# Low weight halves moved from VectorE to GpSimd, and high halves one block earlier on ScalarE, around the output projections of a two-block transformer kernel

## The chip, the cores and the metric

One NeuronCore of a Trainium2 chip runs the whole program. The metric is the device time of one execution in microseconds (us). The kernel before took 1125.66 us, the median of three runs (1124.29 to 1127.17).

## What is computed

Two transformer blocks over 512 tokens of width 1024, in float32. What matters here is the end of each sublayer: an output projection, a post-norm added to the residual, a pre-norm, and the next matrix product.

```python
h = h + rmsnorm(mix, norm_mix_post[l])            # boundary 0
z = rmsnorm(h, norm_mlp_pre[l]) @ w_up[l]
ff = jnp.square(jax.nn.relu(z)) @ w_down[l]
h = h + rmsnorm(ff, norm_mlp_post[l])             # boundary 1
...
    h = rms_norm(x, pre_norm[layer])
    y = even_mixer(h, ...)  /  odd_mixer(h, ...)
    x = x + rms_norm(y, post_norm[layer])         # boundaries 2 and 3
```

## The kernel before, in words

Every float32 product is made of three fast ones. A number is kept as a high half (rounded to the reduced format) and a low half (the number less its high half), and `mm3` issues high by high, high by low and low by high (lines 702 to 704). So each 1024 x 512 chunk of weights, loaded by SyncE in two pieces of 1 MB into `wl`, is split twice. ScalarE copies the piece into `wh` (`hi(n, piece)`, line 1362, 128x2048). VectorE subtracts it from `wl` and writes the low half over the raw weights as `wlr` (`lo(n, piece)`, line 1768, 128x2048, both inputs in SBUF). TensorE waits for `wlo_done` to reach the count of the piece (`weights`, from `token_tile` and `channel_tile`). There are two slots; chunk n uses slot n % 2, and its load waits until chunk n - 2 has been used.

Chunks are numbered in order of use: N_O1 (second half of the first output projection), then N_UP; the last down chunk, then N_GA; N_AO1, then N_AB. Each pair meets at a boundary, s = 0, 1 and 2. There TensorE makes the projection for four blocks of 128 tokens (24 matmuls each), and for each block b the others do the norms in token-major layout:

- ScalarE (`boundary_blocks`, line 1408): the sum of squares of the block (`half_square`, L1376), the post scale (L1383, L1385), then, in blocks 1 and 2, `hi` of the following chunk, then `pre_scale` (L1391, L1394, L1396: the sum of squares of the new residual and its root), then the high half of the block before, turned (`hi_turned`, L1403).
- VectorE (`boundary_blocks`, line 1826): at s = 1 the last partial sum (`add_down`, L1825), `half_gained` (L1780, from PSUM; at s = 1 L1778, from SBUF), the new residual `rt` (`new_resid`, L1795, 128x1024), in blocks 2 and 3 `lo` of the following chunk, the low half of the block before (`lo_turned`, L1812, from PSUM), and the normed block `un` (`normed`, L1804, 128x1024). L1795 and L1804 read two tensors of SBUF.
- TensorE turns the normed block into channel-major layout (`turn_block`, L840): blocks 0 and 1 inside the tiles of the projection, blocks 2 and 3 inside the tiles of the next chunk at s = 0 and 1 (N_UP, N_GA: token-major products), and by themselves at s = 2, where every tile of N_AB needs all four blocks.

Each engine works through its list in the order in which it is written, and semaphores order the engines. GpSimd has nothing to do at the three boundaries: its list goes from the first mixer's steps to a memset (L1276) before the second mixer's, and from these to the memsets of `glu` (L1282) and the conv sums. Its one subtraction of a whole weight piece is in the first mixer (`split(1)`, L1231, 128x2048). The counter `wlo_done` is bare: it says how many pieces are done and not which, so its increments must come in the order of the pieces.

Of the kernel before, what the change touches and what calls it, by code (L numbers as in the profile page):

```python
# [5 lines left out]
F32 = mybir.dt.float32  # L6
F32R = mybir.dt.float32r
I32 = mybir.dt.int32
ALU = mybir.AluOpType
# [47 lines left out]
N_O0, N_O1, N_UP, N_GA, N_KV, N_Q, N_U, N_GB = 0, 1, 2, 18, 19, 20, 21, 22  # L57
N_AO0, N_AO1, N_AB, N_G0, N_G1, N_CO0, N_CO1 = 23, 24, 25, 29, 30, 31, 32
# [54 lines left out]
def chunk_width(n):  # L113
    return CW if n == N_KV else 2 * CW


def piece_count(n, piece):

    return 2 - piece if n == N_O0 else 2 * n + piece + 1
# [90 lines left out]
def block_kernel(nc, a, out):  # L210
    ctx = ExitStack()
    with ctx:
# [138 lines left out]
        wl = [at("wl0", [P, KT, 512], raw_off), at("wl1", [P, KT, 512], hi_off)]  # L351
        wlr = [at("wlr0", [P, KT, 512], raw_off, F32R), at("wlr1", [P, KT, 512], hi_off, F32R)]
# [852 lines left out]
        @block.gpsimd  # L1205
        def _(pool):
            chain = Chain(pool, pool_step)
            pool.memset(eps[:, :], EPS).then_inc(eps_set, 1)
            pool.wait_ge(eps_set, 1)
            chain.link(pool.memset(relw[32:33, :], -1e30))  # L1210
            pool.memset(gate_w[:, :, :], 0.0).then_inc(gatew_set, 1)
            pool.wait_ge(gatew_set, 1)

            def sum_squares(n):

                for k in range(KT - 1):
                    pool.wait_ge(sq_done, 8 * n + k + 1)
                    if k == 0:
                        if n >= 1:
                            pool.wait_ge(rsum_done, n)  # L1220
                        pool.tensor_copy(sq_sum[:, :], sq[:, k % 2, :]).then_inc(sqsum_done, 1)
                    else:
                        pool.wait_ge(sqsum_done, 7 * n + k)
                        pool.tensor_tensor(sq_sum[:, :], sq_sum[:, :], sq[:, k % 2, :], ALU.add)\
                            .then_inc(sqsum_done, 1)

            def split(c):

                pool.wait_ge(hi_done, c + 1)
                pool.wait_ge(lo_done, c)  # L1230
                pool.tensor_tensor(w_lo[:, c % 2, :, :], raw[:, c % 2, :, :], w_hi[:, c % 2, :, :].bitcast(F32),  # L1231
                                   ALU.subtract).then_inc(lo_done, 1)

            def mixer_step_pool(layer, step):
                what, i = step[0], step[1]
                k = 16 * layer + i
                if what == "gla_scaled":

                    d, t = i % 2, i // 2
                    pool.wait_ge(evac_done, 10 + t)  # L1240
                    pool.wait_ge(eb_done, i + 1)
                    if d == 0:
                        pool.wait_ge(enb_done, i + 1)
                        pool.tensor_tensor(kint(d, t), ka[:, t, :], gx[:, :], ALU.mult).then_inc(kint_done, 1)
                    pool.wait_ge(ek_done, i + 1)
                    pool.tensor_tensor(bb[:, :], ka[:, t, :], gl[:, :], ALU.mult).then_inc(ks_done, 1)
                    if d == 1:
                        pool.wait_ge(ks_done, i + 1)
                        pool.tensor_tensor(kint(d, t), ka[:, t, :], gx[:, :], ALU.mult).then_inc(kint_done, 1)
                elif what == "gla_dS" and i == 0:  # L1250
                    pool.wait_ge(vtok_done, 1)
                    pool.wait_ge(pv_done, STEPS)
                    pool.memset(Am[:, :, :, :], 0.0).then_inc(Am_set, 1)
                elif what == "pool_window":

                    pool.wait_ge(evD_done, evacs_before(TILE_AT[N_U, i], "D") + 1)
                    if i == 0:
                        pool.wait_ge(upad_set, 1)
                        pool.wait_ge(mix2_in, 16 * MIX2_LOADS)
                    else:  # L1260
                        pool.wait_ge(pooled_done, i)
                    src = uu[:, i, :]
                    for m in range(i + 1):
                        sh, lo = 1 << m, (2 << m) - 1
                        dst = wsum[:, m % 2, :]
                        chain.link(pool.tensor_tensor(dst[:, lo:], src[:, lo:], src[:, lo - sh:UPAD + TOK - sh], ALU.add))
                        src = dst
                    pool.tensor_tensor(src[:, UPAD:UPAD + 16], src[:, UPAD:UPAD + 16], wcnt[:, i, :], ALU.mult)\
                        .then_inc(wsum_done, 1)

            split(1)
            sum_squares(0)
            for step in STEPS_OF[0]:
                mixer_step_pool(0, step)
            pool.wait_ge(wtile_done, CHUNK_END[N_GA - 1])
            pool.memset(uu[:, :, 0:UPAD], 0.0).then_inc(upad_set, 1)  # L1276
            for step in STEPS_OF[1]:
                mixer_step_pool(1, step)
            pool.wait_ge(ob_done, 4)

            for slot in range(4):
                pool.memset(glu[:, slot, 0:CPAD], 0.0).then_inc(pad_set, 1)  # L1282
            for t in range(KT):
                for m in range(1, ACT_TAPS + 1):
                    made = PRODUCTS * t + m + 1
                    pool.wait_ge(prod_done, made)
                    g = made - 1
                    if m == 1:
                        if t >= 2:
                            pool.wait_ge(conv_done, t - 1)  # L1290
                        pool.tensor_tensor(pacc[:, t % 2, :], prod[:, (g - 1) % 4, :], prod[:, g % 4, :], ALU.add)\
                            .then_inc(padd_done, 1)
                    else:
                        pool.wait_ge(padd_done, ACT_TAPS * t + m - 1)
                        pool.tensor_tensor(pacc[:, t % 2, :], pacc[:, t % 2, :], prod[:, g % 4, :], ALU.add)\  # L1295
                            .then_inc(padd_done, 1)
# [3 lines left out]
        def _(act):  # L1300
# [57 lines left out]
            def hi(n, piece):  # L1358

                slot, kk, cols = n % 2, slice(4 * piece, 4 * piece + 4), slice(0, chunk_width(n))  # L1360
                act.wait_ge(wraw[slot][piece], 16 * sum(chunk_dmas(q) for q in range(slot, n + 1, 2)))
                act.activation(wh[slot][:, kk, cols], wl[slot][:, kk, cols], ACT.Copy).then_inc(whi_done, 1)  # L1362
# [43 lines left out]
            def boundary_blocks(s, following):  # L1406

                for b in range(NBLK):
                    half_square(s, 1, b)
                    post_scale(s, b)  # L1410
                    if b in (1, 2):
                        hi(following, b - 1)
                    pre_scale(s, b)
                    if b >= 1:
                        hi_turned(s, b - 1)
                hi_turned(s, NBLK - 1)
# [293 lines left out]
        def _(dve):  # L1710
# [53 lines left out]
            def lo(n, piece):  # L1764

                slot, kk, cols = n % 2, slice(4 * piece, 4 * piece + 4), slice(0, chunk_width(n))
                dve.wait_ge(whi_done, piece_count(n, piece))
                dve.tensor_tensor(wlr[slot][:, kk, cols], wl[slot][:, kk, cols], wh[slot][:, kk, cols].bitcast(F32),  # L1768
                                  ALU.subtract).then_inc(wlo_done, 1)
# [37 lines left out]
            def lo_turned(s, b):  # L1807

                for g in range(2):
                    dve.wait_ge(hiT_done, 2 * (NBLK * s + b) + g + 1)  # L1810
                    cols = slice(b * P, (b + 1) * P)
                    dve.tensor_tensor(act_lo[:, 4 * g:4 * g + 4, cols], psT[:, g, :].rearrange("p (k n) -> p k n", k=4),  # L1812
                                      act_hi[:, 4 * g:4 * g + 4, cols].bitcast(F32), ALU.subtract)\
                       .then_inc(loT_done, 1)
# [12 lines left out]
            def boundary_blocks(s, following):  # L1827

                for b in range(NBLK):
                    if s == 1:  # L1830
                        add_down(3, 1, b)
                    half_gained(s, 1, b)
                    new_resid(s, b)
                    if b >= 2:
                        lo(following, b - 2)
                    if b >= 1:
                        lo_turned(s, b - 1)
                    normed(s, b)
                lo_turned(s, NBLK - 1)

            def mixer_step_dve(layer, step):
                what, i = step[0], step[1]
# [386 lines left out]
```

## Time and profile before

| | |
|---|---|
| median of three runs | 1125.66 us |
| the profiled execution | 1125.93 us |
| its span, first to last instruction | 1124.1 us |
| TensorE busy | 1033.6 us (92%) |
| VectorE busy | 584.4 us (52%) |
| ScalarE busy | 468.5 us (42%) |
| GpSimd busy | 170.0 us (15%) |
| mean granted TensorE clock | 0.960 of full |

TensorE is busy nearly throughout, so time is lost where it stands still or runs at the lower clock. Matmuls overlap: one 128x512 matmul is recorded as 0.39 us, and the next starts 0.23 us after it.

### The profile page before, as it was taken

Reading aid. Unit: us, or ns where it says so; the run is one execution under the profiler, and the core shown is the slowest. Engines: PE = TensorE matmul, PEld = TensorE weight load, DVE = VectorE, ACT = ScalarE, POOL = GpSimd, SP = SyncE. Lnnn points to the kernel's source line nnn. Section 1 sums busy time; section 2 is a strip of 40 time slices with the busy share of each in tenths; the row PEclk is TensorE's granted clock in tenths of the full one; section 3 lists DMA queues with packets and bytes.
Section 4 is the critical chain, followed back from the end, with each engine's and each line's share of the span. In section 5 each row is a group of like instructions: output and inputs, shape, how many; then the busy total and the mean of one; then the engine's idle time right before and its main releaser. Section 6 shows DMA issues by size and latency. Waiting matters only on the chain.

```text
span 1124.1 us, 12285 instructions
## 1 busy us (share of the span) xinstructions
PE 1033.6 (92%) x4847; PEld 824.7 (73%) x4847; DVE 584.4 (52%) x768; ACT 468.5 (42%) x765; POOL 170.0 (15%) x131
## 2 busy tenths in 40 slices
PE   3899999997999999999999979989898899979897
PEld 2677677886788888888888868767677667657676
DVE  5436665235744234333344463366556397777853
ACT  3325562135533334134123354234355557556541
POOL 2200101000000000000000000022000189886300
PEclk8999999998999999999999999989999799999989
DMA  6532102034221252233224214302033222210301
GB/s 213 73 122 76 38 1 76 1 113 150 76 76 75 75 187 75 75 109 116 76 75 149 76 38 132 141 1 75 2 136 120 68 76 76 75 54 27 145 1 75
DMA packets 55823, 93.91 MB, mean 84 GB/s; under 512 B 2581, under 2 KB 23958, under 8 KB 55638
## 3 DMA queue, kind: packets, MB, share of 16 engines
q1 hardware_dynamic: 53648, 90.61, 23.3%
q10 hardware_dynamic: 2118, 2.52, 1.6%
q8 instruction: 39, 0.64, 0.2%
q14 instruction: 18, 0.15, 0.0%
HBM read 90.76 MB, written 2.36 MB: 83 GB/s over the span
## 4 chain that ended last, share of the span: by engine, by line
PE 55%; DVE 8%; ACT 4%; issue 3%; POOL 1%; DMA 1%; SPq 0%; DVEq 0%; POOLq 0%; ACTq 0%
PE acc L702 17%; PE acc L703 17%; PE acc L704 16%; DVE wlr L1768 2%; ACT wh L1362 2%; DVE psT L2113 1%; POOL pacc L1295 1%; PE psT L861 1%; DMA wl<-in_c_w_in_dram 1%; PE ps L861 1%; PE ps L993 1%; DVE rt L1795 1%; DVE act_lo L1812 1%; ACT junk L1391 1%; PE psT L978 1%
## 5 line engine op out<-in xcount | busy, mean ns | idle before, releaser
L1768 DVE TENSOR_TENSOR wlr<-wl,wh 128x2048 fp32r<-128x2048 f32 (+1 forms) x66 | 149.9, 2276 | 96.4 <-ACT wh L1362 96.4
L702 PE MATMUL acc<-act_hi,wh 128*128 128x512 f32 x464 | 187.9, 405 | 1.7 <-DVE act_lo L1812 1.4
L704 PE MATMUL acc<-act_hi,wlr 128*128 128x512 f32 x464 | 182.3, 393 | 0.0
L703 PE MATMUL acc<-act_lo,wh 128*128 128x512 f32 x464 | 182.1, 392 | 0.0
L1362 ACT ACTIVATE wh<-wl 128x2048 fp32r<-128x2048 f32 (+1 forms) x66 | 123.7, 1880 | 61.2 <-DMA wl<-in_w_up_dram 35.1
L702 PE MATMUL acc<-wh,act_hi 128*128 128x512 f32 x320 | 131.3, 410 | 19.0 <-DVE act_lo L1738 7.6
L703 PE MATMUL acc<-wlr,act_hi 128*128 128x512 f32 x320 | 127.6, 399 | 0.0
L704 PE MATMUL acc<-wh,act_lo 128*128 128x512 f32 x320 | 127.6, 399 | 0.0
L1295 POOL TENSOR_TENSOR pacc<-pacc,prod 128x512 f32<-128x512 f32 x80 | 117.5, 1469 | 28.6 <-ACT prod L1644 16.1
L702 PEld LDWEIGHTS acc<-act_hi,wh 128*128 128x128 f32 x464 | 88.4, 191 | 21.7 <-DVE act_lo L1812 1.8
L703 PEld LDWEIGHTS acc<-act_lo,wh 128*128 128x128 f32 x464 | 88.3, 190 | 19.1 <-issue 1.7
L704 PEld LDWEIGHTS acc<-act_hi,wlr 128*128 128x128 f32 x464 | 87.9, 190 | 19.0
L703 PE MATMUL acc<-wlr,hid_hi 128*128 128x512 f32 x256 | 100.8, 394 | 0.0
L702 PE MATMUL acc<-wh,hid_hi 128*128 128x512 f32 x256 | 100.5, 393 | 0.0
L704 PE MATMUL acc<-wh,hid_lo 128*128 128x512 f32 x256 | 99.4, 388 | 0.0
L702 PEld LDWEIGHTS acc<-wh,act_hi 128*128 128x128 f32 x320 | 61.9, 194 | 34.9 <-DVE act_lo L1738 9.3
L702 PE MATMUL acc<-act_hi,w_hi 128*128 128x512 f32 x152 | 65.5, 431 | 10.8 <-DVE act_lo L1730 7.4
L1276 POOL MEMSET uu<- 128x64 f32 x1 | 0.2, 157 | 475.5 <-PE acc L704 475.5
L703 PEld LDWEIGHTS acc<-wlr,act_hi 128*128 128x128 f32 x320 | 62.3, 195 | 13.0 <-issue 0.7
L704 PEld LDWEIGHTS acc<-wh,act_lo 128*128 128x128 f32 x320 | 61.9, 193 | 13.5
L1644 ACT ACTIVATE prod<-glu,taps 128x512 f32<-128x512 f32 x88 | 60.0, 716 | 13.7 <-POOL pacc L1295 13.0
L2113 DVE SCALAR_TENSOR_TENSOR psT<-glu,taps,psT 128x512 f32<-128x512 f32 x83 | 59.7, 750 | 4.7 <-PE psT L861 4.4
(221 smaller groups left out, 1536.8 us busy)
## 6 DMA issues: line engine op xcount, KB each, us to landing
wl<-in_w_up_dram SPq DMA_DIRECT2D x16, 1024.0 KB, 6.3
wl<-in_w_down_dram SPq DMA_DIRECT2D x16, 1024.0 KB, 6.3
raw<-in_w_in_dram SPq DMA_DIRECT2D x18, 512.0 KB, 4.8
wl<-in_a_w_in_dram SPq DMA_DIRECT2D x8, 1024.0 KB, 6.2
wl<-in_c_w_in_dram SPq DMA_DIRECT2D x16, 512.0 KB, 6.2
wl<-in_w_out_dram SPq DMA_DIRECT2D x4, 1024.0 KB, 6.2
wl<-in_ab_w_out_dram SPq DMA_DIRECT2D x4, 1024.0 KB, 7.4
wl<-in_c_w_in_dram SPq DMA_DIRECT2D x4, 1024.0 KB, 6.4
```

Source lines behind the costliest of these rows:

```text
L702: pe.matmul(dst, hi, x_hi, start=first, stop=False)
L703: pe.matmul(dst, hi, x_lo, start=False, stop=False)
L704: return pe.matmul(dst, lo, x_hi, start=False, stop=last)
L861: last = pe.matmul(vacc(t, 0), diag[:, t % 2, m, :], glu[:, t % 4, j:j + TOK], start=m == 0, stop=m == PE_TAPS - 1)
L978: last = pe.transpose(psTf[:, (2 * b + j) * P:(2 * b + j + 1) * P], LG[layer][:, i % 2, j, 1 + b * P:1 + (b + 1) * P], ident[:, :])
L993: last = pe.matmul(ps6[:, 64 * j:64 * j + 64], PT[layer][:, (2 * b + j) * P:(2 * b + j + 1) * P], VTOK[layer][:, kb, 64 * g:64 * g + 64], ...
L1295: pool.tensor_tensor(pacc[:, t % 2, :], pacc[:, t % 2, :], prod[:, g % 4, :], ALU.add)\
L1362: act.activation(wh[slot][:, kk, cols], wl[slot][:, kk, cols], ACT.Copy).then_inc(whi_done, 1)
L1391: act.activation(junk[:, :], rt[:, b, :], ACT.Square, accum_out=ssq[:, s, 16 + b:17 + b])\
L1644: act.activation(prod[:, g % 4, :], glu[:, t % 4, j:j + TOK], ACT.Copy, scale=taps[:, t, j:j + 1])\
L1768: dve.tensor_tensor(wlr[slot][:, kk, cols], wl[slot][:, kk, cols], wh[slot][:, kk, cols].bitcast(F32), ALU.subtract).then_inc(wlo_done, 1)
L2113: ins = dve.scalar_tensor_tensor(out=sums, in0=src, scalar=taps[:, t, m:m + 1], in1=sums, op0=ALU.mult, op1=ALU.add)
```

## The change

In each boundary s = 0, 1, 2 the low halves of the following chunk are taken out of VectorE's list and made by GpSimd. GpSimd waits, for each piece, for its high half and for all earlier increments of `wlo_done`. VectorE waits at the end of the boundary for both pieces, so that its own next increment comes after them. At s = 0 and 1 ScalarE makes the high halves in blocks 0 and 1 in place of 1 and 2; at s = 2 they stay where they were.

```diff
+            def lo_following(n):
+                for piece in range(2):
+                    kk, cols = slice(4 * piece, 4 * piece + 4), slice(0, chunk_width(n))
+                    pool.wait_ge(whi_done, piece_count(n, piece))
+                    pool.wait_ge(wlo_done, piece_count(n, piece) - 1)
+                    pool.tensor_tensor(wlr[n % 2][:, kk, cols], wl[n % 2][:, kk, cols],
+                                       wh[n % 2][:, kk, cols].bitcast(F32), ALU.subtract).then_inc(wlo_done, 1)
...
             for step in STEPS_OF[0]:
                 mixer_step_pool(0, step)
+            lo_following(N_UP)
+            lo_following(N_GA)
             pool.wait_ge(wtile_done, CHUNK_END[N_GA - 1])
...
             for step in STEPS_OF[1]:
                 mixer_step_pool(1, step)
+            lo_following(N_AB)
             pool.wait_ge(ob_done, 4)
...
                     post_scale(s, b)
-                    if b in (1, 2):
-                        hi(following, b - 1)
+                    if b in ((1, 2) if s == 2 else (0, 1)):
+                        hi(following, b - (s == 2))
                     pre_scale(s, b)
...
                     new_resid(s, b)
-                    if b >= 2:
-                        lo(following, b - 2)
                     if b >= 1:
                         lo_turned(s, b - 1)
                     normed(s, b)
                 lo_turned(s, NBLK - 1)
+                dve.wait_ge(wlo_done, piece_count(following, 1))
```

## Rows read from the trace of the kernel before

**Rows 1.** Timeline of TensorE, boundary 0: start us, us, engine, line, operation, [idle before].

```profile
303.11 0.79 PE L702 MATMUL acc<-wh,act_hi 128*128 128x512 f32 x1 [2.37 <-DVE wlr L1768]
310.19 1.03 PE L840 MATMUL psT<-ident_ones,un 128*128 128x128 f32 x8
```

**Rows 2.** Timeline of TensorE, boundary 1.

```profile
667.49 0.50 PE L702 MATMUL acc<-wh,act_hi 128*128 128x512 f32 x1 [4.40 <-DVE wlr L1768]
674.70 1.04 PE L840 MATMUL psT<-ident_ones,un 128*128 128x128 f32 x8
```

**Rows 3.** Timeline of TensorE, boundary 2.

```profile
874.41 1.97 PE L840 MATMUL psT<-ident_ones,un 128*128 128x128 f32 x8 [5.64 <-DVE un L1804]
```

**Rows 4.** Busy time by stretch; PEclk is the granted clock, the last columns DMA share and GB/s.

```profile
280.00:281.00 1.00, 1.00 (x6) 0.84 (x5) 0.91 (x2) 0.28 (x2) 0.00 (x0) 1.00 0.78 285
304.00:305.00 1.00, 1.00 (x4) 0.71 (x4) 1.00 (x2) 0.00 (x0) 0.00 (x0) 0.50 0.26 82
```

**Rows 5.** Timeline of VectorE, boundary 0.

```profile
283.62 1.28 DVE L1804 SCALAR_TENSOR_TENSOR un<-rt,stat,gpre 128x1024 f32<-128x1024 f32 x1 [1.78 <-ACT stat L1396]
...
290.88 1.27 DVE L1804 SCALAR_TENSOR_TENSOR un<-rt,stat,gpre 128x1024 f32<-128x1024 f32 x1
...
292.85 1.28 DVE L1795 SCALAR_TENSOR_TENSOR rt<-yg,stat,rt 128x1024 f32<-128x1024 f32 x1
294.05 2.28 DVE L1768 TENSOR_TENSOR wlr<-wl,wh 128x2048 fp32r<-128x2048 f32 x1
...
297.60 1.28 DVE L1804 SCALAR_TENSOR_TENSOR un<-rt,stat,gpre 128x1024 f32<-128x1024 f32 x1
```

**Rows 6.** Timeline of ScalarE, boundary 0.

```profile
280.10 0.20 ACT L1385 ACTIVATE stat<-stat 128x1 f32<-128x1 f32 x1
...
285.65 1.90 ACT L1362 ACTIVATE wh<-wl 128x2048 fp32r<-128x2048 f32 x1
```

**Rows 7.** Timeline of GpSimd and VectorE where both are at work, four meetings.

```profile
20.39 4.51 POOL L1231 TENSOR_TENSOR w_lo<-raw,w_hi 128x2048 fp32r<-128x2048 f32 x1 [18.83 <-ACT w_hi L1327]
21.00 4.45 DVE L1730 SCALAR_TENSOR_TENSOR act_lo<-resid,vec,act_hi 128x512 fp32r<-128x512 f32 x1 [2.75 <-ACT act_hi L1349]
...
150.79 1.30 POOL L1246 TENSOR_TENSOR sq_sum<-ka,sq 128x512 f32<-128x512 f32 x1
150.81 1.31 DVE L1929 COPY decay<-eb 128x8 f32<-128x8 f32 x1
...
916.27 2.29 DVE L1768 TENSOR_TENSOR wlr<-wl,wh 128x2048 fp32r<-128x2048 f32 x1
916.37 3.33 POOL L1295 TENSOR_TENSOR pacc<-pacc,prod 128x512 f32<-128x512 f32 x1
...
924.69 1.26 POOL L1295 TENSOR_TENSOR pacc<-pacc,prod 128x512 f32<-128x512 f32 x1
925.28 0.69 DVE L2093 TENSOR_TENSOR glu<-acc,sg 128x512 f32<-128x512 f32 x1
```

**Rows 8.** Timeline of ScalarE (first row) and VectorE, boundary 1.

```profile
646.92 1.91 ACT L1362 ACTIVATE wh<-wl 128x2048 fp32r<-128x2048 f32 x1
...
652.15 1.28 DVE L1804 SCALAR_TENSOR_TENSOR un<-rt,stat,gpre 128x1024 f32<-128x1024 f32 x1
...
660.48 1.27 DVE L1804 SCALAR_TENSOR_TENSOR un<-rt,stat,gpre 128x1024 f32<-128x1024 f32 x1
...
668.70 1.28 DVE L1804 SCALAR_TENSOR_TENSOR un<-rt,stat,gpre 128x1024 f32<-128x1024 f32 x1
```

**Rows 9.** Timeline of ScalarE (first two rows) and VectorE, boundary 2.

```profile
854.38 1.90 ACT L1362 ACTIVATE wh<-wl 128x2048 fp32r<-128x2048 f32 x1
...
860.72 1.90 ACT L1362 ACTIVATE wh<-wl 128x2048 fp32r<-128x2048 f32 x1
...
859.60 1.28 DVE L1804 SCALAR_TENSOR_TENSOR un<-rt,stat,gpre 128x1024 f32<-128x1024 f32 x1
...
861.58 1.29 DVE L1795 SCALAR_TENSOR_TENSOR rt<-yg,stat,rt 128x1024 f32<-128x1024 f32 x1
```

## The prediction, made before the changed kernel was run

> **What bounds the kernel now.** I read the page first, then TensorE's waits, then its timeline at the three boundaries, then the other engines there. TensorE sets the end; only its idle time and its low clock can be won or lost. At boundary 0 it waits 2.37 us for the second low piece of N_UP; the matmul behind the wait takes 0.79 us where others take 0.39, and block 3 is turned at 310.19 [rows 1]. In the stretch behind the wait the granted clock is 0.50 [rows 4], the lower of its levels, 1.2 of 2.4 GHz; 24 matmuls at 0.227 us and nothing else would have brought the turn at 308.6, so the low clock costs 1.6 us. At boundary 1 the wait for the low piece is 4.40 us and block 3 is turned at 674.70 [rows 2], with the same 1.6 us inside. At boundary 2 TensorE waits for no weights: it waits 5.64 us for `un` of block 3 [rows 3]. So the low pieces end TensorE's wait at two boundaries, and the chain of norms between VectorE and ScalarE at the third.
>
> **What the move takes away.** Six subtractions of 2.28 us leave VectorE. They do not lie on the chain of norms: at boundary 0 `lo` starts at 294.05, as `rt` of block 2 ends, and VectorE would otherwise stand idle, since `un` at 297.60 has to await ScalarE's root of that `rt` and the turned halves [rows 5]. So I take 0 for the chain from removing them. What they free is TensorE's second half tile. ScalarE's copies one block sooner: the first starts behind the scale of block 0, at 280.2 in place of 285.65 [rows 6], and ends at 282.1. Its transfer is there: the 2 MB of the chunk are in before 281 (the last stretch with traffic moves 285 GB/s) [rows 4], and the first piece goes first. It pushes the root of block 0 by 0.15 us; the second copy takes the place in block 1 that the first had; block 2 has none, which is worth under 0.2 us.
>
> **What GpSimd takes for it, and what that blocks.** One 128x2048 subtraction took GpSimd 4.51 us [rows 7]. Two follow each other with at least 0.9 us between the end of the one and VectorE's next claim, so both would be ready before TensorE asks; GpSimd is idle otherwise, and nothing queued behind (a memset, the `glu` memsets) is due before VectorE's own wait is over. VectorE's new wait at the boundary's end I therefore cost at nothing: the pieces are done some 10 us before. The price is elsewhere. While that 4.51 us subtraction ran, VectorE's 128x512 operation on two tensors of SBUF took 4.45 us (like forms take 0.69) and ended 0.55 us behind GpSimd: it waited for the whole of it. A copy that started 0.02 us behind a GpSimd sum also waited it out (1.31 us), and where VectorE had started first, by 0.10 us, GpSimd waited: 3.33 us for a sum of 1.28. A VectorE operation with one input from PSUM was untouched (0.69 us beside a GpSimd sum) [rows 7]. So I take an exclusive claim for a whole instruction, first come first served. At the boundaries `rt` and `un` read two tensors of SBUF and must wait; `half_gained` from PSUM and `lo_turned` need not. The Trainium skill, "SBUF — State Buffer", section "Who interferes with whom", has the same rule; "Advanced Engine Details and Errata", "VectorE Performance Modes", names only VectorE's two-port modes as blocked, by which these operations would run free and the first rival below would come true. The row of 4.45 us speaks for the former.
>
> **Boundary 0.** First GpSimd piece: 282.25 to 286.76. `un` of block 0 asks at 283.8 (0.15 behind 283.62 [rows 5]), waits, and ends 1.15 us (its 1.28 less the 0.13 that the blocked row saves) after GpSimd: 287.91, 3.0 later than now. The second copy ends at 287.55 [rows 6]; the second piece asks at 287.7, gets the port at 287.9 and holds it until 292.28. `rt` of block 1 asks at 288.6 (`half_gained` lies between) and ends at 293.43. From the end of an `rt` to the start of its `un` are 3.47 us (294.13 to 297.60), and from `un` to `un` 6.72 (290.88 to 297.60) [rows 5], in both cases with ScalarE between. So `un` of block 1 starts at 296.9 (now 290.88), of block 3 at 310.34, and ends at 311.6. TensorE waits 0.9 us for block 0 and 4.0 us for block 1 (turn at 298.2); behind that wait I charge one low clock spell, 1.6 us, as now. Its own path is then 298.2 + turn 0.8 + 24 matmuls 5.4 + 1.6 = 306.05, + turn 0.8 + 5.4 = 312.3 for the turn of block 3, against 310.19: **+2.1**. Without the spell VectorE is later, 311.7: +1.5.
>
> **Boundary 1.** The same sequence delays `un` of block 0 by 3.0, and with it the sum, the square and the second copy: 649.9 to 651.8 (now 646.92 [rows 8]). The second piece runs from 652.0 to 656.46. `rt` of block 1 is through before it; `un` of block 1 asks at 655.15 (652.15 + 3.0), waits, and ends at 657.61, 4.2 later than now. The next two follow at 8.2 us each (660.48 to 668.70 [rows 8]): `un` of block 3 ends at 674.0. TensorE has its weights early and is ready for this turn at 672.1, or 673.7 with a low spell, so it turns at 674.1 against 674.70 [rows 2]: **-0.6**. The stall has changed hands and not size. If a further spell of low clock falls behind the turn, add 1.4: +0.8 is the other end.
>
> **Boundary 2.** The copies stay, so the first piece runs 856.42 to 860.93 (copy ends at 856.28, and 0.14 to start as in the row of 20.39 [rows 7, 9]). `un` of block 1 asks at 859.60 [rows 9] and ends at 862.08 in place of 860.88. `rt` of block 2 asks 0.70 behind that (861.58 against 860.88 now), at 862.78. The second copy ends at 862.62, so GpSimd asks at 862.76. The two ask within 0.02 us. If GpSimd has it, `rt` ends at 862.76 + 4.51 + 1.15 = 868.42 against 862.87, and everything behind moves by **+5.5**. If VectorE has it, GpSimd runs 864.06 to 868.43, and `un` of block 2, asking at 867.5, ends at 869.58 against 867.63: +1.9. I take the first, since GpSimd is ahead by the hair that sufficed in the copy's row. The clock is low there already, so I add nothing for it.
>
> **Sum.** 2.1 - 0.6 + 5.5 = +7.0 on the profiled execution's 1125.93 us: 1132.9. The median of the runs is 0.27 lower. The rest of the kernel hangs on TensorE's progress and moves as a whole; I cost it at 0.
>
> **Rivals.** (1) *No claim conflict for these forms.* `un` and `rt` run at full speed beside GpSimd. Then boundary 0 loses its wait of 2.37 us, the 1.6 us of low clock behind it and some 0.2 at the restart: turn at 306.0, which `un` of block 3, ending at 305.6 (304.32 + 1.28, one period of 6.72 behind 297.60), just allows, 4.2 us sooner; boundary 1 is held by `un` of block 3, which ends at 669.98 (668.70 + 1.28 [rows 8], +0.25), turn at 670.2, 4.5 sooner; boundary 2 stays. 1125.93 - 8.7 = 1117.2, faster. It decides at the first `un` of boundary 0: 1.3 us or 4.1. Against it: the 4.45 us row and the 3.33. For it: no `un` or `rt` was seen beside GpSimd. Chance 0.08. (2) *VectorE wins the claim at boundary 2*: 2.1 - 0.6 + 1.9 = +3.4, 1129.3; with the spell at boundary 1, 1130.7. For it: VectorE's time comes from differences of 0.02 us, any of which can turn. Chance 0.37. (3) *The move does not do what it says*: GpSimd's pieces come later than TensorE wants them. With ends at 292.3 and 656.5 against needs at 301 and 661 it has 5 us to spare at least; it would take sums twice as long. It would add the lateness to (2): some 1134. Chance 0.05. (4) *Claims interleave in GpSimd's disfavour*, VectorE always served first: each piece is then delayed by at most the 1.3 us of an operation and the chains by nearly nothing, 1119 to 1127. Chance 0.07. My forecast has the remaining 0.43.
>
> **How the numbers follow.** The forecast's own range is 1131.5 (boundary 0 at +1.5, less rounding) to 1134.8 (boundary 1 at +0.8, and 0.5 for spread). Rival 2 reaches down to 1128.5. The range 1127.5 to 1135.5 leaves out rival 1 and most of 4. About 0.3%, 3.4 us, is what a measurement of this kernel can tell from no change. Slower by more: my forecast, rival 3, and half of rival 2: 0.66. Within it: the rest of 2 and half of 4: 0.23. Faster by more: rival 1 and part of 4: 0.11.
>
> **What would show it.** In the changed profile: `un` (L1804) of block 0 at boundaries 0 and 1 taking 4.1 us and more, `rt` (L1795) of block 1 at boundary 0 taking 4.8; GpSimd's subtractions at 4.5 us each with TensorE waiting for L1804 and never for `wlr`; turns of block 3 near 312 and 676 (674.1 plus the 2.1 carried); at boundary 2 either `rt` of block 2 at 5.6 us or `un` of block 2 at 2.1. I am wrong if L1804 and L1795 stay at 1.28 us while GpSimd works.

## The result, and the profile after

The changed kernel takes 1129.63 us, the median of seven runs (1127.91 to 1134.01), against 1125.66 (1124.29 to 1127.17) before, of seven runs too: ratio 1.0041, 95% interval 1.0024 to 1.0058. It is slower, by 4.0 us. The profiled execution has a span of 1127.8 us.

First the busy times from the page of the changed kernel, then GpSimd's and TensorE's waits there (waiting engine and line, releaser, us in total, times, longest):

```profile
PE 1032.1 (92%) x4847; PEld 823.5 (73%) x4847; DVE 588.1 (52%) x762; ACT 468.7 (42%) x765; POOL 198.2 (18%) x137
```

```profile
POOL wlr L1240 <- ACT wh L1374: 542.1, 6, 352.4
...
PE psT L840 <- DVE un L1816: 21.8, 7, 6.6
```

VectorE has six instructions fewer and is busy 3.7 us longer. TensorE's waits for `wlr` of VectorE, 7.0 us in all before, are gone at the boundaries, and its waits for `un` went from 7.3 us in three to 21.8 in seven. The stall changed its name and grew.

Boundary 0 on GpSimd, then on VectorE (they answer to [rows 5]; this execution reaches the boundary 0.51 us later than the one before):

```profile
282.71 4.62 POOL L1240 TENSOR_TENSOR wlr<-wl,wh 128x2048 fp32r<-128x2048 f32 x1 [100.38 <-ACT wh L1374]
288.14 4.73 POOL L1240 TENSOR_TENSOR wlr<-wl,wh 128x2048 fp32r<-128x2048 f32 x1 [0.81 <-ACT wh L1374]
```

```profile
284.26 4.15 DVE L1816 SCALAR_TENSOR_TENSOR un<-rt,stat,gpre 128x1024 f32<-128x1024 f32 x1 [1.91 <-ACT stat L1408]
288.33 0.68 DVE L1792 TENSOR_TENSOR yg<-acc,gpost 128x512 f32<-128x512 f32 x1
289.10 4.85 DVE L1807 SCALAR_TENSOR_TENSOR rt<-yg,stat,rt 128x1024 f32<-128x1024 f32 x1
...
297.42 1.27 DVE L1816 SCALAR_TENSOR_TENSOR un<-rt,stat,gpre 128x1024 f32<-128x1024 f32 x1
```

`un` of block 0 asks at 284.26, while GpSimd is at work until 287.33, and ends at 288.41, 1.08 behind it. GpSimd's second piece asks at 288.14, is held a little by that `un` (4.73 in place of 4.62), and then holds `rt` of block 1 until 293.95, again 1.08 behind GpSimd's end at 292.87. The operation between, L1792, has one of its two inputs in PSUM and takes its usual 0.68 beside GpSimd.

Boundary 2 on GpSimd, then on VectorE (they answer to [rows 9]), with TensorE's two late turns ([rows 3]):

```profile
856.99 4.63 POOL L1240 TENSOR_TENSOR wlr<-wl,wh 128x2048 fp32r<-128x2048 f32 x1 [81.91 <-ACT wh L1374]
863.33 4.58 POOL L1240 TENSOR_TENSOR wlr<-wl,wh 128x2048 fp32r<-128x2048 f32 x1 [1.71 <-ACT wh L1374]
```

```profile
860.23 2.46 DVE L1816 SCALAR_TENSOR_TENSOR un<-rt,stat,gpre 128x1024 f32<-128x1024 f32 x1
862.62 0.68 DVE L1792 TENSOR_TENSOR yg<-acc,gpost 128x512 f32<-128x512 f32 x1
863.40 5.58 DVE L1807 SCALAR_TENSOR_TENSOR rt<-yg,stat,rt 128x1024 f32<-128x1024 f32 x1
```

```profile
873.78 1.97 PE L840 MATMUL psT<-ident_ones,un 128*128 128x128 f32 x8 [6.56 <-DVE un L1816]
880.51 1.97 PE L840 MATMUL psT<-ident_ones,un 128*128 128x128 f32 x8 [4.76 <-DVE un L1816]
```

GpSimd asked 0.07 us ahead of `rt` of block 2, and `rt` took 5.58 us.

### The profile page after: what moved, and what is told of

It reads as the page before. It is cut to its first block, busy times and chain, and to the rows that moved or that the text cites. A ratio compares the mean times of both kernels' runs of the same rounds, so it can differ in the third digit from the quotient of the medians.

```text
span 1127.8 us, 12294 instructions
## 1 busy us (share of the span) xinstructions
PE 1032.1 (92%) x4847; PEld 823.5 (73%) x4847; DVE 588.1 (52%) x762; ACT 468.7 (42%) x765; POOL 198.2 (18%) x137
## 4 chain that ended last, share of the span: by engine, by line
PE 55%; DVE 9%; ACT 4%; issue 3%; POOL 2%; DMA 1%; SPq 0%; DVEq 0%; POOLq 0%; ACTq 0%
PE acc L702 16%; PE acc L703 16%; PE acc L704 16%; POOL pacc L1307 2%; DVE psT L2124 1%; ACT wh L1374 1%; DVE wlr L1780 1%; PE psT L861 1%; DMA wl<-in_c_w_in_dram 1%; DVE rt L1807 1%; DVE un L1816 1%; PE ps L861 1%; PE psT L840 1%; DVE act_lo L1824 1%; PE ps L993 1%
## 5 line engine op out<-in xcount | busy, mean ns | idle before, releaser
L1780 DVE TENSOR_TENSOR wlr<-wl,wh 128x2048 fp32r<-128x2048 f32 (+1 forms) x60 | 137.3, 2293 | 93.6 <-ACT wh L1374 93.6
L1240 POOL TENSOR_TENSOR wlr<-wl,wh 128x2048 fp32r<-128x2048 f32 x6 | 27.8, 4627 | 542.1 <-ACT wh L1374 542.1
```

The costliest lines, as they stand in the source:

```text
L1240: pool.tensor_tensor(wlr[n % 2][:, kk, cols], wl[n % 2][:, kk, cols], wh[n % 2][:, kk, cols].bitcast(F32), ALU.subtract).then_inc(wlo_done, 1)
```

## The experiments

To compare boundaries whatever came before them, I take each from the start of ScalarE's first square of block 0 to TensorE's turn of block 3, and two other stretches: from that turn at boundary 1 to the first square of boundary 2 (the second mixer), and from the turn at boundary 2 to the end of the span (the rest). These five are from the timeline of one profiled execution each, in us; the median is of all runs of the kernel. Its ratio to the kernel before stands in the section of the kernel.

```
kernel                 b. 0    b. 1   mixer 2   b. 2   rest    median
before                31.13   35.52   173.08   26.63  249.69   1125.66
changed               33.56   34.85   171.44   32.10  247.29   1129.63
vector_sooner         27.01   30.82   171.51   26.62  249.60   1114.17
gpsimd_quarters       27.71   32.38   172.83   27.47  248.94   1120.30
gpsimd_halves         29.19   33.01   173.97   29.92  249.85   1126.21
high_alone            31.02   35.48   173.08   26.62  249.71   1126.04
boundary2_undone      33.55   34.84   174.31   26.62  249.92   1128.24
boundary2_only        31.03   35.48   173.06   32.10  247.54   1128.61
behind_rt             33.53   34.84   174.18   28.86  247.40   1128.79
delay_alone           31.22   35.51   173.15   31.51  248.42   1130.14
changed_again         33.56   34.84   174.26   32.09  248.22   (1132.18)
before_again          31.19   35.49   173.14   26.62  249.71   (1124.87)
```

The last two are single executions. The kernel before had a median of 1125.36 where vector_sooner, the quarters, the halves and boundary2_undone were run, of 1126.45 beside high_alone, boundary2_only, behind_rt and delay_alone, and of 1125.58 beside the last three; each ratio is to the one beside it.

Two stretches are not in the table. Between boundaries 0 and 1 lie 328.99 us before and in the changed kernel alike. The way to boundary 0, which is the same program in all of them, takes 277.4 to 279.7 us: 279.06 in the profiled execution before, 279.57 in that of the changed kernel.

### The low halves left on VectorE, one block sooner

```diff
-                    if b >= 2:
-                        lo(following, b - 2)
+                    if b in ((2, 3) if s == 2 else (1, 2)):
+                        lo(following, b - (2 if s == 2 else 1))
```

on the kernel before, with ScalarE's part of the change and nothing on GpSimd.

> High halves one block sooner at boundaries 0 and 1, low halves on VectorE too but one block sooner (blocks 1 and 2), no GpSimd at the boundaries; boundary 2 as in the kernel before. Theory (the low halves cost the norm chain nothing on VectorE, the port claim of GpSimd is the whole price): rt and un stay at 1.28 us, block 3 is turned some 4.2 us sooner at boundary 0 and 4.5 sooner at boundary 1 than in the kernel before, no wait of TensorE for wlr is left there; about 1117 us, 1115 to 1120 with low clock spells falling otherwise. Rival (VectorE's load sits in the chain, and GpSimd relieved it): block 3 is turned no sooner than before, 1125 us or more.

1114.17 us, ratio 0.990 (0.9887 to 0.9912): 11 us faster than the kernel before and 15 than the changed one. Boundary 0 of this kernel on VectorE:

```profile
282.06 1.28 DVE L1804 SCALAR_TENSOR_TENSOR un<-rt,stat,gpre 128x1024 f32<-128x1024 f32 x1 [1.90 <-ACT stat L1396]
...
284.31 1.28 DVE L1795 SCALAR_TENSOR_TENSOR rt<-yg,stat,rt 128x1024 f32<-128x1024 f32 x1
285.51 2.28 DVE L1768 TENSOR_TENSOR wlr<-wl,wh 128x2048 fp32r<-128x2048 f32 x1
287.99 1.29 DVE L1812 TENSOR_TENSOR act_lo<-psT,act_hi 128x512 fp32r<-128x512 f32 x2 [0.19 <-ACT act_hi L1403]
289.20 1.28 DVE L1804 SCALAR_TENSOR_TENSOR un<-rt,stat,gpre 128x1024 f32<-128x1024 f32 x1
```

The subtraction sits in the gap behind `rt`, and VectorE still waits 0.19 us for ScalarE after it: it costs the norm chain nothing, and TensorE waits for `wlr` at neither boundary. The boundaries are 4.1 and 4.7 us shorter than before (4.2 and 4.5 were expected). So the low halves had to come sooner, not from another engine. The median gained 2.4 us more than these; 1.6 of them lie in the second mixer of the profiled execution (171.51 against 173.08), see below. It beats both kernels.

### High halves sooner, low halves as before

```diff
-                    if b in (1, 2):
-                        hi(following, b - 1)
+                    if b in ((1, 2) if s == 2 else (0, 1)):
+                        hi(following, b - (s == 2))
```

on the kernel before.

> The kernel before with the high halves of N_UP and N_GA one block sooner, low halves left on VectorE in blocks 2 and 3. Theory (the low halves' place in VectorE's list is what TensorE waits for): TensorE waits for wlr as before, 2.4 us at boundary 0 and 4.4 at boundary 1, block 3 is turned within 0.3 us of the kernel before; no change, 1124 to 1127. Rival (the sooner high halves are the gain of the version with both sooner): 1117 or less.

1126.04 us, ratio 0.9996 (0.9987 to 1.0005), all five distances within 0.11 us of the kernel before, and TensorE's waits for `wlr` are as before (6.9 us in three, 7.0 before). ScalarE's part alone does nothing; the rival is out.

### GpSimd's subtraction in smaller instructions

```diff
-                    pool.tensor_tensor(wlr[n % 2][:, kk, cols], wl[n % 2][:, kk, cols],
-                                       wh[n % 2][:, kk, cols].bitcast(F32), ALU.subtract).then_inc(wlo_done, 1)
+                    for k in range(4 * piece, 4 * piece + 4, 1):
+                        kk = slice(k, k + 1)
+                        ins = pool.tensor_tensor(wlr[n % 2][:, kk, cols], wl[n % 2][:, kk, cols],
+                                                 wh[n % 2][:, kk, cols].bitcast(F32), ALU.subtract)
+                    ins.then_inc(wlo_done, 1)
```

on the changed kernel, for the quarters; for the halves, two instructions of two k each.

> The changed kernel with each GpSimd subtraction issued as four of 128x512. Theory (the port is held for one instruction): no un or rt takes more than 1.28 + 1.3 us, and with the long waits gone block 3 is turned about 3 us sooner than before at boundaries 0 and 1 and 1 to 2 later at boundary 2: about 1121 us, 1118 to 1125. Rival (VectorE is held off for as long as GpSimd has work queued, or GpSimd's reads slow it in proportion): un of block 0 still takes about 4.1 us at both boundaries and the time stays at the changed kernel's 1129.6.

> The changed kernel with each GpSimd subtraction issued as two of 128x1024. Theory (one instruction, one claim): the longest un or rt takes 1.28 + 2.3 = 3.6 us, none takes 4 or more; time between the quarters and the changed kernel, about 1125. Rival (claim for the whole queue of work): as the changed kernel, 1129.6, with un of block 0 at 4.1 us.

Quarters: 1120.30, ratio 0.9954 (0.9939 to 0.9969), faster than before. Halves: 1126.21, 1.0006 (0.9997 to 1.0015). Boundary 0 of the quarters on GpSimd, then `un` of block 0 on VectorE; then `rt` of block 1 in the halves:

```profile
282.18 1.30 POOL L1242 TENSOR_TENSOR wlr<-wl,wh 128x512 fp32r<-128x512 f32 x1 [100.34 <-ACT wh L1377]
283.43 1.30 POOL L1242 TENSOR_TENSOR wlr<-wl,wh 128x512 fp32r<-128x512 f32 x1
284.68 2.29 POOL L1242 TENSOR_TENSOR wlr<-wl,wh 128x512 fp32r<-128x512 f32 x1
286.94 2.27 POOL L1242 TENSOR_TENSOR wlr<-wl,wh 128x512 fp32r<-128x512 f32 x1
```

```profile
283.73 2.08 DVE L1819 SCALAR_TENSOR_TENSOR un<-rt,stat,gpre 128x1024 f32<-128x1024 f32 x1 [1.90 <-ACT stat L1411]
```

```profile
286.54 2.66 DVE L1810 SCALAR_TENSOR_TENSOR rt<-yg,stat,rt 128x1024 f32<-128x1024 f32 x1
```

The same work with 18 more instructions, and `un` waits 0.8 us where it waited 2.9: it asks at 283.73, during the second quarter, and is done 1.08 behind that quarter's end; the third quarter then waits for it (2.29). The longest of `un` and `rt` at boundary 0 are 2.08 (quarters), 2.66 (halves), 4.85 (whole), and over all boundaries 2.09, 3.27 and 5.58. The delay follows the length of one GpSimd instruction and not the amount of work queued, as the claim for a whole instruction says. The number expected of the halves, 1125, was near; the sum of their boundaries is 1.2 us under the kernel before and the median 0.9 over.

### Boundary 2 by itself, both ways

Undone in the changed kernel (the subtraction back on VectorE for s == 2, `lo_following(N_AB)` out), and done alone in the kernel before.

> The changed kernel with boundary 2 put back (low halves of N_AB on VectorE in blocks 2 and 3). Theory: from the first square of block 0 to the turn of block 3 boundary 2 takes as long as in the kernel before, 5.5 us less than in the changed kernel; in all 1124, or 1122 to 1127 if the low clock spells behind it fall otherwise. Rival (boundary 2 costs nothing net, since what it adds comes back in the stage of the convolution): 1129 to 1130, with the saving gone by the end.

> The kernel before with the move made at boundary 2 alone. Theory (port claim of a whole instruction, GpSimd first by a hair): rt of block 2 takes 5.6 us and un of block 1 some 2.4, the turn of block 3 comes 5.5 us later; in the total the same as the delay alone, within 1.5 us. Rival (VectorE gains the race in most runs): rt of block 2 at 1.28 us, un of block 2 at some 2.3, boundary 2 longer by 2 us.

Boundary 2 is 26.62 us when undone (26.63 before) and 32.10 when done alone (32.10 changed): +5.47 belongs to it wholly. In the totals it is worth much less. Undone: 1128.24, ratio 1.0020 (1.0008 to 1.0031), only 1.4 us under the changed kernel and above the expected 1122 to 1127; its profiled execution reaches boundary 2 later by 2.9 us of second mixer, in code that is the same in both kernels. Alone: 1128.61, ratio 1.0023 (1.0014 to 1.0032), 2.2 us over the kernel before. The rest behind it is 2.15 us shorter than before, as in the changed kernel (2.40). The stretches of its profile leave +3.3; why the medians show 1.1 us less is open.

### The second piece held until `rt` of block 2 is done

```diff
+                    if n == N_AB and piece == 1:
+                        pool.wait_ge(res_done, NBLK * 2 + 3)
```

> The changed kernel in which GpSimd starts the second piece at boundary 2 only behind the residual of block 2. Theory (first to ask has the port): rt of block 2 back at 1.28 us, un of block 2 waits instead for the end of the piece, 2 to 2.5 us, and boundary 2 is 3.4 us shorter than in the changed kernel: 1125 to 1128 in all. Rival (GpSimd's work costs VectorE the same wherever it falls): boundary 2 as long as in the changed kernel.

GpSimd, then VectorE, boundary 2:

```profile
865.38 4.55 POOL L1242 TENSOR_TENSOR wlr<-wl,wh 128x2048 fp32r<-128x2048 f32 x1 [3.24 <-DVE rt L1809]
```

```profile
863.92 1.28 DVE L1809 SCALAR_TENSOR_TENSOR rt<-yg,stat,rt 128x1024 f32<-128x1024 f32 x1
...
868.68 2.33 DVE L1818 SCALAR_TENSOR_TENSOR un<-rt,stat,gpre 128x1024 f32<-128x1024 f32 x1
```

`rt` is back at 1.28, `un` of block 2 waits instead, and the boundary is 28.86 us, 3.2 shorter than in the changed kernel: rival 2's case made by hand, +2.2 over the kernel before where the prediction had +1.9. The total, 1128.79 (ratio 1.0025, 1.0015 to 1.0035), is 2.3 us over the kernel before beside it, where the changed kernel is 4.0 over its own, and a little above the expected 1125 to 1128.

### The delay without GpSimd

```diff
+                    if s == 2 and b == 2:
+                        dve.wait_ge(uT_done, 2 * (NBLK * s + 1))
+                        for _ in range(7):
+                            chain.link(dve.tensor_tensor(un[:, 0, 0:512], gpost[:, 0:512], gpre[:, 0:512], ALU.mult))
                     new_resid(s, b)
```

> The kernel before with seven linked 128x512 products put on VectorE ahead of the residual of block 2 at boundary 2 (some 5.5 us; they change nothing in the result), GpSimd as before. Theory (the 3 us that the changed kernel got back lie in where the low clock spells of TensorE fall, and any delay there gets them): boundary 2 is longer by 5 to 6 us, the low clock behind it ends sooner after the restart, the spell near 958 us is gone or moved, and the run is 2.5 to 4 us over the kernel before, not 5.5. Rival (VectorE relieved of the low halves gives them back): the whole 5.5 us stay, 1131.

The seven products lengthen boundary 2 by 4.88 us, and the rest gives back 1.27; the median is 1130.14, 3.7 us over the kernel before, inside the expected 2.5 to 4, ratio 1.0031 (1.0020 to 1.0042). Part of that lies in the restart of TensorE behind the boundary. The stretches in which the lower clock ends, of the kernel before, of this one and of the changed kernel (window, its length, busy time by engine, granted clock, DMA share, GB/s):

```profile
883.00:884.00 1.00, 1.00 (x5) 0.79 (x4) 0.00 (x0) 0.00 (x0) 0.00 (x0) 0.91 0.00 0
887.00:888.00 1.00, 1.00 (x5) 0.80 (x4) 0.00 (x0) 0.00 (x0) 0.00 (x0) 0.81 0.00 0
887.00:888.00 1.00, 1.00 (x5) 0.82 (x4) 0.00 (x0) 0.00 (x0) 0.00 (x0) 0.88 0.00 0
```

A granted clock of 0.91 over a microsecond means 0.2 us at 0.5 and the others at 1. So the kernel before is at the lower clock until 883.2, 8.8 us behind its turn of block 3; this one until 887.4, 7.3 us behind (turn at 880.08); the changed one until 887.2, 6.7 us behind. By an estimate from these, 1.5 and 2.1 us less at half the clock are worth some 0.7 and 1.0 us. So a part of what the changed kernel gets back is got by a plain delay too. The other half microsecond of the 1.27 is not traced. The expectation had the low clock near 958 us gone or moved; it is still there (962.5 to 965.9, 82 us behind the turn, where the kernel before has it 84 behind), and the further 1.1 us that the rest of the changed kernel gives back do not come with the delay.

### The changed kernel and the kernel before, once more

> The changed kernel once more, one profile. Theory (the low clock spells of TensorE in the second mixer and near 960 us fall by chance from execution to execution): the boundaries repeat to 0.2 us (rt of block 2 at boundary 2 again 5.6 us), while the time from the turn of block 3 at boundary 1 to the first square of block 0 at boundary 2 (171.4 us) or from the turn of block 3 at boundary 2 to the end (247.3) comes out 1 us or more off. Rival (both belong to the program): both repeat within 0.3 us.

> The kernel before once more, one profile. Theory (chance): one of the two distances, 173.1 and 249.7 us, comes out 1 us or more off. Rival (they belong to the program): both repeat within 0.3 us.

The boundaries repeat to 0.1 us in both. The kernel before repeats in the mixer and in the rest (173.14 and 249.71), so the expectation missed there; only the way to boundary 0 was 1.2 us shorter. The changed kernel does not repeat: its second mixer takes 174.26 in place of 171.44, and the rest 248.22 in place of 247.29. Stretches of the changed kernel and then of its second execution (window, its length, busy time by engine, granted clock, DMA share, GB/s):

```profile
742.00:750.00 8.00, 6.40 (x26) 4.58 (x24) 5.67 (x9) 2.95 (x6) 1.47 (x2) 0.79 0.00 1
750.00:757.00 7.00, 5.46 (x34) 4.51 (x36) 4.94 (x13) 3.27 (x10) 0.99 (x3) 1.00 0.00 0
960.00:968.00 8.00, 5.94 (x19) 3.27 (x18) 7.96 (x13) 2.77 (x4) 7.28 (x6) 1.00 0.00 0
```

```profile
742.00:750.00 8.00, 4.71 (x22) 3.21 (x22) 5.74 (x10) 2.62 (x7) 2.35 (x3) 0.96 0.00 0
750.00:757.00 7.00, 6.01 (x22) 5.01 (x21) 3.13 (x8) 3.15 (x10) 0.00 (x0) 0.56 0.00 0
960.00:968.00 8.00, 5.94 (x16) 3.26 (x15) 8.00 (x11) 3.92 (x6) 7.28 (x6) 0.79 0.00 0
```

Of this program's three low clock spells in the second mixer, the first lasted 3.4 us the first time (743.9 to 747.3) and 6.8 the second (749.3 to 756.1), as the granted clocks of 0.79, 0.96 and 0.56 give it; near 960 it had none and then one of 3.4. The kernel before has the spell there too:

```profile
955.00:963.00 8.00, 5.92 (x12) 2.41 (x12) 7.96 (x13) 3.17 (x5) 7.28 (x6) 0.79 0.00 0
```

That one program differs so from execution to execution is shown for the changed kernel, by two of them. The Trainium skill, "TensorE: Matmul & The Clock Gate", "Part 1: The HAM clock gate", says that the number of matmuls which one kernel runs at the low clock differs from run to run; the trace agrees, with 3.4 and 6.8 us of low clock in the same place. But chance is not all of it. The spell near 960 is in every profiled execution whose boundary 2 is as before, and in those of the delay, the quarters and the halves; it is missing in three of the four that have whole GpSimd instructions at boundary 2 (changed, boundary2_only, behind_rt). And the kernels whose boundary 1 is as before all have 173.1 us of second mixer, the others 171.4 to 174.3. Why is not settled.

### GpSimd at work without reading

The version of the first experiment, and at boundary 0 two fills behind each high copy, into a tensor that is not in use there:

```diff
+            for piece in range(2):
+                pool.wait_ge(whi_done, piece_count(N_UP, piece))
+                pool.wait_ge(og_out, 4)
+                for part in range(2):
+                    pool.memset(hid_hi[:, 4 * part:4 * part + 4, :].bitcast(F32), 0.0).then_inc(probe_done, 1)
+                    pool.wait_ge(probe_done, 2 * piece + part + 1)
...
+                act.wait_ge(probe_done, 4)
```

> The version with both halves sooner on VectorE and ScalarE, and at boundary 0 four fills of 128x2048 on GpSimd, two behind each high copy: GpSimd works 1.8 us four times over, but reads nothing. Theory (what meets is the reading of a second SBUF tensor by VectorE and of SBUF by GpSimd): un of block 0 and wlr beside the fills stay at 1.28 and 2.29 us, the time at 1114. Rival (any GpSimd work shuts such VectorE operations out): un of block 0 takes 2 us and more, wlr waits too.

GpSimd, then VectorE:

```profile
282.81 1.82 POOL L1280 MEMSET hid_hi<- 128x2048 f32 x1 [100.49 <-ACT wh L1369]
284.68 1.81 POOL L1280 MEMSET hid_hi<- 128x2048 f32 x1
288.30 1.81 POOL L1280 MEMSET hid_hi<- 128x2048 f32 x1 [1.81 <-issue]
```

```profile
284.38 1.28 DVE L1812 SCALAR_TENSOR_TENSOR un<-rt,stat,gpre 128x1024 f32<-128x1024 f32 x1 [1.90 <-ACT stat L1403]
...
287.83 2.28 DVE L1776 TENSOR_TENSOR wlr<-wl,wh 128x2048 fp32r<-128x2048 f32 x1
```

`un` starts inside one fill and ends inside the next, at 1.28 us; a fill starts inside the subtraction and both keep their time. Boundary 0 is 27.00 us, as without the fills (27.01), the time 1115.61, ratio 0.9917 (0.9886 to 0.9949). So GpSimd's writing alone holds nothing up; what the subtraction has beyond it is its reading. The Trainium skill, "SBUF — State Buffer", "Who interferes with whom", says this too, of VectorE instructions with two inputs in SBUF.

## Why the prediction was right, and where its sum was off

**Direction and mechanism: right.** The forecast was a whole-instruction claim that makes `un` and `rt` wait. `un` of block 0 took 4.15 us at boundaries 0 and 1 (4.1 said), `rt` of block 1 at boundary 0 4.85 (4.8 said), `rt` of block 2 at boundary 2 5.58 (5.6 said). The quarters and the halves exclude a claim for all work queued, the fills exclude GpSimd at work without reading.

**Size: its own range missed.** The forecast by itself ran from 1131.5 to 1134.8 (its terms, 1.5 - 0.6 + 5.5 on the median, give 1132.1 for the lower end). The measured 1129.63 lies below; it is inside the wide range only because that took in rival 2, and it is nearest to rival 2's 1129.3. The total alone would have spoken for the wrong mechanism. The `rt` of 5.58 us decides it.

**Boundary 0:** +2.43 measured, +2.1 said. VectorE's chain came as forecast, and so did TensorE's turn of block 1 (298.75, which is 298.24 without the 0.51 by which this execution is later; 298.2 said). The 0.3 lie in TensorE's own path from there to the turn of block 3: 14.38 us, summed as 14.1.

**Boundary 1:** -0.67 measured, -0.6 said. TensorE waits for `un` where it had waited for `wlr`.

**Boundary 2:** +5.47 measured, +5.5 said, and GpSimd gained the race in all three profiled executions in which it was run, by 0.07 us. The forecast had called it by 0.02 us with a chance of 0.37 against it. Rival 2 did not happen; made by hand it is worth 3.2 us at the boundary.

**The moved low halves cost the chain nothing on VectorE:** shown by the first experiment, which keeps them there.

**The step that failed** is the last of the sum: "The rest of the kernel hangs on TensorE's progress and moves as a whole; I cost it at 0." The profiled executions add up: the boundaries give +7.23, the way to boundary 0 +0.51, the stretch between boundaries 0 and 1 nothing, the second mixer -1.64, the rest -2.40, together +3.70, which is the difference of the spans; the medians differ by 3.97. Of the 2.40, about 1.0 is the sooner end of the low clock behind the restart (an estimate, see the delay), of which a plain delay gets a part as well. The rest was 1.5 us shorter in the second execution too (249.69 less 248.22), and 2.15 with boundary 2 alone. What is left goes with the spell near 960 us, which was absent in the first execution and present in the second. The -1.64 of the mixer did not repeat: the second execution had +1.2 (174.26 against 173.08), and boundary2_undone and behind_rt had +1.2 and +1.1, all three with the longer spell. That is of the size of the spread of the runs: 6.1 us from first to last, where the kernel before has 2.9. The second execution, with its boundaries the same, took 1132.18, close to the 1132.9 forecast; the median did not. How often each course of the low clock falls, and so how much of the median's missing 3 us is owed to which, is open. By these runs the term should have been -1 to -2.4 for what lies behind boundary 2, with 1.5 us to either side for the mixer.

**Rival 1** (no claim conflict, 1117.2) had the right price for what sooner low halves are worth: with them on VectorE the boundaries gave 4.1 and 4.7, where it said 4.2 and 4.5.

## What to carry to other kernels

Before moving work to an idle GpSimd, list which VectorE operations on the critical chain read two tensors of SBUF (and copies: the one of [rows 7] waited too), and compare the length of one GpSimd instruction with their slack: each waits for the whole of the instruction in progress. If it must go there, issue it in short instructions; better, look first for a gap on the engine that has it, since a wait for an operation may mean only that it stands too late in its list. A delay ahead of a phase at the low clock need not be paid in full (here 1.3 of 4.9 us came back), and a single profiled execution can be off by 3 us by where its low clock spells fall: compare stretches between two fixed points of the program, and take a second execution.

## What the runs showed of the hardware that I had not expected

A GpSimd fill of 128x2048 (1.81 us) beside VectorE operations on two tensors of SBUF slows neither (1.28 and 2.28 us kept), while a GpSimd subtraction stops them for up to 4.3 us. A lead of 0.07 us decided 4.3 us of waiting, and decided it the same way in three executions out of three. And one program's second mixer took 171.4 or 174.3 us by where TensorE's low clock fell, while its three boundaries repeated to 0.1 us.
